# Latent heads with the mask in free contraction rows and the values' two parts side by side; differential q and k rotated on GpSimd

## The reference, cut to what matters

```python
a_q, a_k, a_v, b_ql, b_kvl, b_kr = split_cols(h @ w_in, AB_IN_SPLITS)
a_q = rope(rms_norm(a_q.reshape(B, S, 2 * A_HEADS, A_QK_DIM), a_q_norm), pos)
a_k = rope(rms_norm(a_k.reshape(B, S, 2 * A_HEADS, A_QK_DIM), a_k_norm), pos)
...
def latent_attention(q_nope, q_rope, k_nope, k_rope, v, scale):
    ...
        s = (jnp.einsum('bqhd,bkhd->bhqk', q_nope[:, lo:hi], k_nope[:, :hi])
             + jnp.einsum('bqhr,bkr->bhqk', q_rope[:, lo:hi], k_rope[:, :hi])).astype(jnp.float32) * scale
        p = masked_softmax(s, mask)
        return jnp.einsum('bhqk,bkhd->bqhd', p.astype(v.dtype), v[:, :hi])
```

## Time and profile before

| | us |
|---|---|
| median of 3 runs | 1278.57 |
| lowest and highest | 1277.1, 1279.0 |
| profiled execution | 1279.58 |
| its span | 1277.8 |

### The profile page before, as it was taken

One profiled execution on the slowest core, in us unless ns is written; L12 is line 12 of the kernel. 1 busy time (PEld: TensorE's weight loads), 2 busy tenths in 40 slices (PEclk: granted clock), 3 DMA queues, 4 the chain that ended last, 5 costly groups with the idle time before them and its releaser, 6 DMA issues.

```text
span 1277.8 us, 16943 instructions
## 1 busy us (share of the span) xinstructions
PE 1253.7 (98%) x6308; PEld 1064.7 (83%) x6308; DVE 569.3 (45%) x995; ACT 583.9 (46%) x959; POOL 528.7 (41%) x267
## 2 busy tenths in 40 slices
PE   8999989999999999999999999999999999999999
PEld 8899968888888888888878888887888888888887
DVE  7856568553221022222288887887232210122210
ACT  5767756454322122223377878885443221222320
POOL 4656411175445344445432222222744444344442
PEclk9999989999999999999999999999999999999999
DMA  5221100033333222232221111110332332222331
GB/s 204 88 66 51 51 34 19 15 128 101 97 117 114 71 95 97 90 123 94 74 66 50 49 49 66 61 55 17 115 99 99 106 119 75 96 92 92 118 118 42
DMA packets 29143, 105.84 MB, mean 83 GB/s; under 512 B 3360, under 2 KB 3616, under 8 KB 29088
## 3 DMA queue, kind: packets, MB, share of 16 engines
q1 hardware_dynamic: 28944, 105.07, 24.8%
q10 hardware_dynamic: 144, 0.02, 0.0%
...
## 4 chain that ended last, share of the span: by engine, by line
PE 88%; DVE 8%; ACT 1%; issue 1%; POOL 1%; DMA 0%; POOLq 0%
PE bank L346 23%; PE bank L347 22%; PE bank L350 22%; PE bank L1512 3%; PE bank L1543 2%; PE bank L1459 1%; PE bank L1125 1%; PE bank L966 1%; PE bank L970 1%; PE bank L968 1%; PE bank L1074 1%; PE bank L1364 1%; PE bank L1365 1%; PE bank L1054 1%; PE bank L372 1%
## 5 line engine op out<-in xcount | busy, mean ns | idle before, releaser
L335 POOL TENSOR_TENSOR w_lo<-wraw,w_hi 128x1024 fp32r<-128x1024 f32 (+4 forms) x180 | 456.8, 2539 | 687.1 <-ACT w_hi L323 687.1
L346 PE MATMUL bank<-h_hi,w_hi 128*128 128x512 f32 x896 | 350.9, 392 | 0.1
L347 PE MATMUL bank<-h_lo,w_hi 128*128 128x512 f32 x896 | 349.0, 389 | 0.0
L323 ACT ACTIVATE w_hi<-wraw 128x1024 fp32r<-128x1024 f32 (+4 forms) x180 | 198.2, 1102 | 243.6 <-DVE x L671 125.6
L350 PE MATMUL bank<-h_hi,w_lo 128*128 128x512 f32 x896 | 221.8, 389 | 0.0
L346 PEld LDWEIGHTS bank<-h_hi,w_hi 128*128 128x128 f32 x896 | 168.2, 188 | 36.2 <-issue 1.1
L350 PEld LDWEIGHTS bank<-h_hi,w_lo 128*128 128x128 f32 x896 | 168.2, 188 | 34.9
L347 PEld LDWEIGHTS bank<-h_lo,w_hi 128*128 128x128 f32 x896 | 168.3, 188 | 34.3
L346 PE MATMUL bank<-f_hi,w_hi 128*128 128x512 f32 x352 | 136.9, 389 | 0.0
L347 PE MATMUL bank<-f_lo,w_hi 128*128 128x512 f32 x352 | 136.9, 389 | 0.0
L634 ACT ACTIVATE f_hi<-fa 128x512 f32 (+1 forms) x44 | 27.8, 633 | 217.2 <-DVE fa L660 217.2
...
## 6 DMA issues: line engine op xcount, KB each, us to landing
...
```

The lines of the kernel that those rows point to most:

```text
L323: nc.scalar.activation(whi[:, s, at:at + width], wraw[:, s, at:at + width], ACT.Copy).then_inc(S("w_hi"), 1)
L335: nc.gpsimd.tensor_tensor(wlo[:, s, at:at + width], wraw[:, s, at:at + width], whi[:, s, at:at + width], ALU.subtract).then_inc(S("w_lo"), 1)
L346: nc.tensor.matmul(out_bank, w, src_hi[kt], start=(kt == 0), stop=False)
L347: nc.tensor.matmul(out_bank, w, src_lo[kt], start=False, stop=False)
```

## The change

**The mask.** The latent heads' q and k use 96 of 128 rows. In the high part of q, row 96 + c now holds 1 where the query is in chunk c, and 0 elsewhere; in the high part of k, row 96 + c holds -1e30 where the key's chunk is later than c. The remaining rows, and those rows of the low parts, hold 0. The score matmuls contract over all 128 rows, and the matmuls with `cmask` are gone from the latent heads (the differential heads keep them). The rows are filled once: a second DMA, two casts and two memsets on VectorE at the start.

**The values.** High and low part of a head's value lie side by side in one tile `vb` (64 + 64 columns). One matmul with the high part of the probabilities gives both products, in output rows 0 to 63 and 64 to 127; a second, with the low part of the probabilities and the high part of the value, adds to rows 0 to 63. So there are two matmuls per key block instead of three. The two halves have to be added: ScalarE copies the lower half to `bo` (`b_lower_act`), VectorE adds (`b_add_dve`), both where the output's high and low part were made before; these are now made from `bo` later in the next head (`b_mhi_act`, `b_mlo_dve`).

**Rotation of q and k.** ScalarE squares a half and then copies it into `qa` or `ka`; VectorE only sums the squares. GpSimd rotates a whole piece in place, in four instructions (`qk_rope_pool`: two products of half the features, one of all, one sum), in heads 1, 3, 5 and 6, ahead of the low part of a weight chunk. `qk_add_pool` is gone, also the one ahead of head 0. Both halves of pieces 2 and 3 are squared and copied at the end of heads 1 and 3; before, the second half was done in heads 2 and 4. GpSimd scales k in heads 5 and 7 instead of 3 and 5, and the first transposes of the differential q and k, and the memsets ahead of them, wait for all four rotations.

```diff
@@ -181,7 +181,7 @@
...
-    (vbhi, vblo), _ = pair("vb", [P, NB, B_HEADS * B_V])
+    vb, _ = place("vb", [P, NB, B_HEADS, 2 * B_V], F32R)
...
@@ -979,35 +982,36 @@
...
         nc.scalar.activation(pj_sq[:, t, :], bank[PJ[t]][:], ACT.Square).then_inc(S("pj_sq"), 1)
+        nc.scalar.activation(qk_of(p)[0][:, p % 2, 2 * t:2 * t + 2, :],
+                             bank[PJ[t]][:].rearrange("p (i n) -> p i n", i=2), ACT.Copy).then_inc(S("pj_c"), 1)
...
-    def qk_dve(dve, p, t):
-
+    def qk_sum_dve(dve, p, t):
+
+        dve.wait_ge(S("pj_sq"), 2 * p + t + 1)
+        nc.vector.reduce_sum(col(t_as(p) + 8 * t, 8), pj_sq[:, t, :].rearrange("p (j n) -> p j n", n=A_DIM),
+                             AX).then_inc(S("pj_sum"), 1)
+
+    ROPE_AT = (1, 3, 5, 6)
+
+    def qk_rope_pool(pool, p):
         dst, tab = qk_of(p)
         s = A_DIM // 2
-        y = bank[PJ[t]][:].rearrange("p (i j n) -> p i j n", i=2, n=A_DIM)
-        u = t2[:, 512 * t:512 * t + 512].rearrange("p (i j n) -> p i j n", i=2, n=A_DIM)
-        o = dst[:, p % 2, 2 * t:2 * t + 2, :].rearrange("p i (j n) -> p i j n", n=A_DIM)
+        o = dst[:, p % 2, :, :].rearrange("p i (j n) -> p i j n", n=A_DIM)
+        u = t2[:].rearrange("p (i j n) -> p i j n", i=NB, n=A_DIM)
 
         def of(a, w):
-            return spread(tab[:, 2 * t:2 * t + 2, a:a + w].rearrange("p i (j n) -> p i j n", j=1), [P, 2, 4, w])
-        if t == 0:
-            dve.wait_ge(S("tabs"), 4)
-            wait(dve, "pj_add", p)
-        dve.wait_ge(S("pj_sq"), 2 * p + t + 1)
-        nc.vector.tensor_tensor(u[:, :, :, 0:s], y[:, :, :, s:2 * s], of(A_DIM, s), ALU.mult)
-        nc.vector.tensor_tensor(u[:, :, :, s:2 * s], y[:, :, :, 0:s], of(A_DIM + s, s), ALU.mult)
-        nc.vector.tensor_tensor(o, y, of(0, A_DIM), ALU.mult).then_inc(S("pj_c"), 1)
-        nc.vector.reduce_sum(col(t_as(p) + 8 * t, 8), pj_sq[:, t, :].rearrange("p (j n) -> p j n", n=A_DIM),
-                             AX).then_inc(S("pj_sum"), 1)
-
-    def qk_add_pool(pool, p):
+            return spread(tab[:, :, a:a + w].rearrange("p i (j n) -> p i j n", j=1), [P, NB, 4, w])
         pool.wait_ge(S("pj_c"), 2 * p + 2)
-        dst, _ = qk_of(p)
-        o = dst[:, p % 2, :, :].rearrange("p i n -> p (i n)")
-        nc.gpsimd.tensor_tensor(o, o, t2[:], ALU.add).then_inc(S("pj_add"), 1)
+        wait(pool, "pj_add", p)
+        nc.gpsimd.tensor_tensor(u[:, :, :, 0:s], o[:, :, :, s:2 * s], of(A_DIM, s), ALU.mult).then_inc(S("pj_t"), 1)
+        nc.gpsimd.tensor_tensor(u[:, :, :, s:2 * s], o[:, :, :, 0:s], of(A_DIM + s, s), ALU.mult).then_inc(S("pj_t"), 1)
+        pool.wait_ge(S("pj_t"), 3 * p + 2)
+        nc.gpsimd.tensor_tensor(o, o, of(0, A_DIM), ALU.mult).then_inc(S("pj_t"), 1)
+        pool.wait_ge(S("pj_t"), 3 * p + 3)
+        nc.gpsimd.tensor_tensor(o, o, u, ALU.add).then_inc(S("pj_add"), 1)
...
@@ -1066,15 +1070,14 @@
...
+            pe.wait_ge(S("cmask"), 5)
...
             for n, (a, c) in enumerate(((bqhi, bkhi), (bqhi, bklo), (bqlo, bkhi))):
-                nc.tensor.matmul(o, a[0:B_QK, b * P:(b + 1) * P], c[0:B_QK, 0:w], start=(n == 0), stop=False,
-                                 skip_group_check=True)
-            last = nc.tensor.matmul(o[:, w - 256:w], ident_r[:], cmask[:, 0 if b == 0 else 1, :], start=False,
-                                    stop=True, skip_group_check=True)
+                last = nc.tensor.matmul(o, a[:, b * P:(b + 1) * P], c[:, 0:w], start=(n == 0), stop=(n == 2),
+                                        skip_group_check=True)
             if b:
                 last.then_inc(S("h_s"), 1)
...
@@ -1119,23 +1122,36 @@
...
         if kb == 0:
-            wait(pe, "h_mlo", u)
-        c = slice(P * (u // 2), P * (u // 2) + P)
-        for n, (a, t) in enumerate(((vbhi, pthi), (vbhi, ptlo), (vblo, pthi))):
-            last = nc.tensor.matmul(bank[OUT][:, TQ[kb]:SEQ], a[:, kb, c], t[:, V_AT[kb]:V_AT[kb] + TW[kb]],
-                                    start=(kb == 0 and n == 0), stop=(kb == NB - 1 and n == 2))
+            wait(pe, "b_add", u)
+        for n, (rows, t) in enumerate(((P, pthi), (B_V, ptlo))):
+            last = nc.tensor.matmul(bank[OUT][0:rows, TQ[kb]:SEQ], vb[:, kb, u, 0:rows],
+                                    t[:, V_AT[kb]:V_AT[kb] + TW[kb]], start=(kb == 0 and n == 0),
+                                    stop=(kb == NB - 1), skip_group_check=True)
         if kb == NB - 1:
             last.then_inc(S("h_o"), 1)
 
-    def b_out_act(act, u):
+    def b_rows(u):
+        return slice(64 * (u % 2), 64 * (u % 2) + 64)
+
+    def b_lower_act(act, u):
         act.wait_ge(S("h_o"), u + 1)
-        r = slice(64 * (u % 2), 64 * (u % 2) + 64)
-        nc.scalar.activation(mhi[r, A_HEADS + u // 2, :], bank[OUT][r, :], ACT.Copy).then_inc(S("h_mhi"), 1)
-
-    def b_out_dve(dve, u):
+        wait(act, "h_mlo", u - 1)
+        nc.scalar.activation(bo[b_rows(u), :], bank[OUT][B_V:P, :], ACT.Copy).then_inc(S("b_lower"), 1)
+
+    def b_add_dve(dve, u):
+        dve.wait_ge(S("b_lower"), u + 1)
+        r = b_rows(u)
+        nc.vector.tensor_tensor(bo[r, :], bank[OUT][0:B_V, :], bo[r, :], ALU.add).then_inc(S("b_add"), 1)
+
+    def b_mhi_act(act, u):
+        act.wait_ge(S("b_add"), u + 1)
+        r = b_rows(u)
+        nc.scalar.activation(mhi[r, A_HEADS + u // 2, :], bo[r, :], ACT.Copy).then_inc(S("h_mhi"), 1)
+
+    def b_mlo_dve(dve, u):
         dve.wait_ge(S("h_mhi"), u + 1)
-        r = slice(64 * (u % 2), 64 * (u % 2) + 64)
-        nc.vector.tensor_tensor(mlo[r, A_HEADS + u // 2, :], bank[OUT][r, :], mhi[r, A_HEADS + u // 2, :],
+        r = b_rows(u)
+        nc.vector.tensor_tensor(mlo[r, A_HEADS + u // 2, :], bo[r, :], mhi[r, A_HEADS + u // 2, :],
                                 ALU.subtract).then_inc(S("h_mlo"), 1)
...
@@ -1268,7 +1284,7 @@
...
-                pe.wait_ge(S("h_mlo"), B_HEADS)
+                pe.wait_ge(S("b_add"), B_HEADS)
...
@@ -1703,6 +1720,8 @@
             for u in range(B_HEADS):
                 if u % 2 == 0 and u < 6:
                     b_pair_pool(pool, u // 2 + 1)
+                if u in ROPE_AT:
+                    qk_rope_pool(pool, ROPE_AT.index(u))
...
@@ -1790,12 +1805,10 @@
...
-                if u in (2, 4):
-                    qk_act(act, 1 + u // 2, 1)
...
                 if u:
-                    b_out_act(act, u - 1)
+                    b_lower_act(act, u - 1)
...
@@ -1810,14 +1823,17 @@
...
+                if u:
+                    b_mhi_act(act, u - 1)
                 hi_static(act, 14 + u)
...
                 if u in (1, 3):
                     qk_act(act, 2 + u // 2, 0)
+                    qk_act(act, 2 + u // 2, 1)
...
-            b_out_act(act, B_HEADS - 1)
+            b_lower_act(act, B_HEADS - 1)
...
@@ -1979,8 +2001,6 @@
...
-                if u in (2, 4):
-                    qk_dve(dve, 1 + u // 2, 1)
...
@@ -1991,10 +2011,13 @@
...
                 for c in range(3):
                     b_pt_dve(dve, u, c)
+                if u:
+                    b_mlo_dve(dve, u - 1)
                 if u == 6:
                     qk_mean_dve(dve, 1)
                 if u in (1, 3):
-                    qk_dve(dve, 2 + u // 2, 0)
+                    qk_sum_dve(dve, 2 + u // 2, 0)
+                    qk_sum_dve(dve, 2 + u // 2, 1)
...
@@ -2238,8 +2263,12 @@
...
+    masks_a = np.zeros((P, 2, 256 + SEQ), f)
+    masks_a[:, 0, :P], masks_a[:, 0, P:256], masks_a[:, 1, P:256] = hidden, BIG, hidden
+    chunk = np.arange(SEQ) // CHUNK
+    for c in range(SEQ // CHUNK):
+        masks_a[B_QK + c, 0, 256:] = chunk == c
+        masks_a[B_QK + c, 1, 256:] = np.where(chunk > c, f(BIG), f(0))
 
...
```

52 lines of the change are left out of this document (29 added, 23 removed).

## The result

The changed kernel takes 1272.05 us (median of 5 runs, 1270.96 to 1272.87), against 1279.0 for the kernel before (1277.1 to 1279.42, 5 runs). The ratio is 0.9948, 95% interval 0.9935 to 0.9962: 7.0 us faster by the medians (6.7 by the ratio), where 4.6 were forecast. The time is inside the stated range. The profiled execution has a span of 1270.3 us against 1277.8.

The account below looks back on a forecast made before the run. Seven latent heads were bound by TensorE's queue, head 7 and what follows by the ScalarE/VectorE chain. Terms -9.0 - 0.3 - 0.2 + 1.3 + 0.3 + 1.6 + 1.7 = -4.6 us gave 1274.0 us as median; range 1269.5 to 1278.5.

Parts of the forecast that it names:

- rival 1: The shared port does not bite: rotation instructions fall beside VectorE's, no stalls, 1270.7 us; chance 0.27.
- TensorE's 1.12 us a head: Latent heads: four mask matmuls (0.48 us) and a third of the value matmuls (0.64) go; -9.0 us over 8 heads.
- Heads 2 and 4: ScalarE's added copies delay VectorE's first maximum to 2.2 us after head start, so TensorE idles; +1.3 us for both heads.
- Before head 0: TensorE's 1.20 us wait at the end of GpSimd's chain mostly stays; -0.2 us, bounds 0 and 1.2.
- The mean waits until about 2.5 into head 7: Head 6's mean of q1 waits for the rotation's last instruction, holding head 7's first maximum to 2.5 instead of 0.9; +1.6 us.
- Nothing waited for them: Heads 2 and 4: removing VectorE's three mid-head multiplies was taken to gain nothing.
- up to +1.7: First differential head: GpSimd's later scaling of k1 holds VectorE's second product of maxima, for which an exponential waits; +1.7 us.
- a change of clock outside the sum: First differential head: 2.2 us less if its half-speed clock goes; up to 2 more if head 7's wait brings another drop.
- The second: Rival: long rotation instructions hit the means in heads 1, 3 and 5, some 0.9 us a head, 1276.7 us; chance 0.15.
- The third: Rival: rotations longer than 7.7 us make head 7's transposes late; slower, 1282 us at 12.5 per rotation; chance 0.06.
- The fourth: Rival: value matmuls get no cheaper because changing between 64 and 128 output rows costs the saving; 1279.1 us; chance 0.03.
- The port's condition in the prediction: A VectorE instruction with two inputs in SBUF waits for the end of the running GpSimd instruction; without this rule 1270.7 us.

Follow-up runs that it names:

- experiment 7: Experiment 3's kernel with, in heads 2 and 4, the squares' sum and output addition behind the maxima, ScalarE's output copy behind the second exponential: 1269.12 us, ratio 0.9923.
- experiment 3: Changed kernel with the mean of the squares of the second q piece moved from the end to the middle of head 6: 1270.37 us, ratio 0.9944.
- experiment 1: Changed kernel with q and k rotated as before, so new mask and values without the rotation on GpSimd: 1278.12 us, ratio 1.0000.
- experiment 2: Kernel before with only the rotation of q and k on GpSimd added: 1278.2 us, ratio 0.9993.
- experiment 6: Changed kernel without the rotation on GpSimd and with the mean of the squares in the middle of head 6: 1275.51 us, ratio 0.9971.
- experiment 10: Kernel before with only the mask put in the free rows of q and k: 1275.71 us, ratio 0.9973.
- experiment 11: Changed kernel with the last rotation moved behind the low part of head 6's weight chunk: 1277.65 us, ratio 0.9992.

## Why the prediction was right, and where not

**The total: near, and in part by luck.** Of the 2.9 us by which the span came out below its forecast, 2.45 lie in the first differential head, where a loss of 1.7 was forecast and 0.75 were gained. The others, up to 0.8 a stretch, partly cancel. And by the time alone, 1272.05 is nearer to rival 1's 1270.7 than to my 1274.0; only the rows tell the two apart.

**TensorE's 1.12 us a head: right.** Heads 1, 3, 5 and 6 together lost 4.29 of 4.5 us.

**Heads 2 and 4: right in mechanism**, 11.24 and 11.22 where 11.3 was forecast; experiment 7 shows the place. The first maximum started 1.76 us after head 2's start, where I had 2.2.

**Before head 0: mis-sized**, -0.96 for -0.2. I followed GpSimd's chain back to its own work and stopped. Its first root waits for VectorE, which had six multiplies fewer. From the first squares of the projection to ScalarE's logarithm for that root it is 11.42 us now (40.37 to 51.79), where it was 11.96 (40.99 to 52.95), and the other profiles give 11.42 to 11.45 with the rotation on GpSimd and 11.96 or 11.97 without. So this term is 0.54. The other 0.4 is not the change: nine kernels of this case, the changed one among them, are the same up to head 0, and their profiles start it anywhere from 69.03 to 70.71.

**Head 7: the right stall, a wrong cause.** "The mean waits until about 2.5 into head 7": the maximum began 2.3 in, behind the rotation's last instruction, as forecast. The whole was 0.45 more than forecast. I had priced only the maximum; ScalarE's copy to `bo` came to stand behind the root that waits for the mean, and the addition waited another 0.55 us for it. That this is the 0.45 is not shown; moving the mean took 1.88 us from the head (experiment 3), where the term was 1.6. And I put the stall on the rotation. Experiments 1, 2 and 6 show that the rotation alone does not cause it, and that mask and values alone do: the output's low part went ahead of the mean, and the mean slipped behind whatever GpSimd starts next.

**"Nothing waited for them"** (VectorE's three multiplies in heads 2 and 4): true of heads of 11.8 us, false of heads of 10.7. This is the step that failed most, though the total could not show it, since the change takes these multiplies away. By my working, mask and values without the rotation would have been the better kernel; experiment 1 measured no gain at all. The rotation makes the room that the saved matmuls need: it is worth 0.5 us in heads 0 to 7 of the kernel before, and 4.6 beside mask and values.

**First differential head: the stall came, the time did not.** The step "up to +1.7" was right up to the transposes (+1.5), but the stretch got 0.75 shorter: behind the transposes it gained 2.26, which the prediction had only as a change of clock outside the sum (2.2). I had added a wait to an unchanged clock. But that is not the wait's doing alone. The mask alone (experiment 10) has no such wait, its transposes come 12.48 us after the head's start as before, and its head is 21.67 us: its low stretch (181.30 to 184.71) was in the old place and half as long. Over all 14 profiles the head is 22.42 to 23.15 us in the five that hold 6.8 us of low clock, and 21.54 to 22.07 in the nine that hold 3.4. So part of the gain, by these ranges some 1 us (an estimate), is that the low stretch was shorter in the one profile of the changed kernel; what made it shorter stays open.

**Rivals.** The port did bite, so the first fell. The second had long instructions under the means in heads 1, 3 and 5: these took 0.99, 0.40 and 0.40 us, instead of 0.16, and TensorE did not wait in those heads. The third was near, with a wait of 0.29 us, and experiment 11 gives its price. The fourth fell by the rows of the values.

**Two readings.** The port's condition in the prediction, two inputs in SBUF, is narrower than its rows. The tensor_scalars at 29.32 have one input in SBUF, and the second of them took 2.39 us instead of 0.17, up to the end of the same GpSimd instruction. So one input in SBUF is no protection by itself; what the runs show free of it are instructions with an input in a bank. And the lower bound for a rotation should have been 6.4 us, not 6.2 (2 x 1.29 + 2 x 1.90); the last one took 7.94 (140.88 to 148.82), where 7.3 was forecast.
